# A fused two-block kernel: modulation work of the feed-forward stage regrouped between DVE and TensorE

## What is computed

```python
# first block (x: 256 x 2048, c: 2048)
mod = silu(c) @ w_ada + b_ada                      # 2048 x 12288
shift1, scale1, gate1, shift2, scale2, gate2 = split(mod, 6)
x = x + gate1 * (concat(s5(...), dilated_attention(...)) @ w_out)
h2 = rms(x, norm2_w) * (1 + scale2) + shift2
x = x + gate2 * ((silu(h2 @ w_ffn_gate) * (h2 @ w_ffn_up)) @ w_ffn_down)    # hidden width 5632
# second block, two layers: attention with a context, then a Fourier mixer
sh, sc, g = split(silu(c_2) @ ada_w_2[i] + ada_b_2[i], 3)                  # 2048 x 6144, i = 0, 1
sh_c, sc_c, g_c = split(silu(c_ctx_2) @ ada_w_2[0] + ada_b_2[0], 3)        # the context, i = 0 only
```

## Time and profile before

| | |
|---|---|
| median of 3 runs | 2595.99 us (2595.85 to 2597.74) |
| profiled execution | 2597.22 us |
| its span, first to last instruction | 2595.4 us |
| mean granted TensorE clock | 0.972 of 2.4 GHz |
| busy: PE / PEld / DVE / ACT / POOL | 2450.6 / 2078.1 / 1652.6 / 1031.9 / 216.2 us |
| moved by DMA | 589.46 MB, mean 227 GB/s |

### The profile page before, as it was taken

One profiled execution on the slowest core, in us unless ns is written; L12 is line 12 of the kernel. 1 busy time (PEld: TensorE's weight loads), 2 busy tenths in 40 slices (PEclk: granted clock), 3 DMA queues, 4 the chain that ended last, 5 costly groups with the idle time before them and its releaser, 6 DMA issues.

```text
span 2595.4 us, 38240 instructions
## 1 busy us (share of the span) xinstructions
PE 2450.6 (94%) x15542; PEld 2078.1 (80%) x15542; DVE 1652.6 (64%) x2005; ACT 1031.9 (40%) x1374; POOL 216.2 (8%) x193
## 2 busy tenths in 40 slices
PE   5899898989999999999999999999968999999995
PEld 1588675569888989888887888888758999999894
DVE  8654644457777788876677566455674484765547
ACT  2453663224333333333343454444423333334431
POOL 0136900011000000000010100000002000000000
PEclk8899899989999999999999999999989999999998
DMA  9853469977999999997553754334544685765551
GB/s 389 311 160 121 134 227 350 381 274 266 350 352 343 366 350 345 340 332 279 155 175 123 223 163 125 100 100 130 177 139 159 199 284 160 242 216 179 155 170 41
DMA packets 278063, 589.46 MB, mean 227 GB/s; under 512 B 20608, under 2 KB 29824, under 8 KB 276608
## 3 DMA queue, kind: packets, MB, share of 16 engines
q1 hardware_dynamic: 277888, 587.02, 65.8%
HBM read 584.85 MB, written 2.10 MB: 226 GB/s over the span
## 4 chain that ended last, share of the span: by engine, by line
PE 86%; DVE 5%; POOL 3%; DMA 3%; issue 2%; ACT 2%; SPq 0%; DVEq 0%; ACTq 0%; POOLq 0%
PE psum L218 12%; PE psum L206 12%; PE psum L219 12%; PE psum L220 12%; PE psum L208 12%; PE psum L207 12%; PE psum L278 4%; DMA start_slots<-in_w_ada 2%; POOL pool_scan_tmp L779 1%; PE psum L2406 1%; PE psum L1794 1%; DVE wlo L195 1%; POOL xacc L779 1%; PE psum L426 1%; PE psum L2382 1%
## 5 line engine op out<-in xcount | busy, mean ns | idle before, releaser
L195 DVE TENSOR_TENSOR wlo<-raw,whi 128x1024 fp32r<-128x1024 f32 (+2 forms) x728 | 881.9, 1228 | 628.6 <-ACT whi L189 626.8
L189 ACT CAST whi<-raw 128x1024 fp32r<-128x1024 f32 (+2 forms) x728 | 736.8, 1022 | 981.9 <-PE psum L220 458.4
L218 PE MATMUL psum<-hh,whi 128*128 128x256 f32 x2688 | 760.5, 283 | 4.9 <-DVE wlo L195 4.4
L220 PE MATMUL psum<-hl,whi 128*128 128x256 f32 x2688 | 750.9, 279 | 0.0
L219 PE MATMUL psum<-hh,wlo 128*128 128x256 f32 x2688 | 750.9, 279 | 0.0
L218 PEld LDWEIGHTS psum<-hh,whi 128*128 128x128 f32 x2688 | 507.7, 189 | 28.1 <-issue 25.9
L220 PEld LDWEIGHTS psum<-hl,whi 128*128 128x128 f32 x2688 | 510.8, 190 | 0.0
L219 PEld LDWEIGHTS psum<-hh,wlo 128*128 128x128 f32 x2688 | 506.7, 188 | 1.6 <-issue 1.0
L206 PE MATMUL psum<-whi,hh 128*128 128x512 f32 (+1 forms) x736 | 301.2, 409 | 17.2 <-DVE wlo L195 14.0
L208 PE MATMUL psum<-whi,hl 128*128 128x512 f32 (+1 forms) x736 | 290.3, 394 | 0.0
L207 PE MATMUL psum<-wlo,hh 128*128 128x512 f32 (+1 forms) x736 | 289.7, 394 | 0.0
(11 more groups left out here) (351 smaller groups left out, 2249.6 us busy)
## 6 DMA issues: line engine op xcount, KB each, us to landing
araw<-in_ada_w SPq DMA_DIRECT2D x128, 512.0 KB, 6.5
raw<-in_w_in_fourier SPq DMA_DIRECT2D x128, 512.0 KB, 3.9
raw<-in_w_ffn_gate SPq DMA_DIRECT2D x88, 512.0 KB, 10.9
raw<-in_w_ffn_up SPq DMA_DIRECT2D x88, 512.0 KB, 7.4
raw<-in_w_ffn_down SPq DMA_DIRECT2D x88, 512.0 KB, 10.6
raw<-in_w_in_attn SPq DMA_DIRECT2D x88, 512.0 KB, 4.4
araw<-in_w_ada SPq DMA_DIRECT2D x80, 512.0 KB, 6.7
start_slots<-in_w_ada SPq DMA_DIRECT2D x64, 512.0 KB, 8.2
```

The costliest lines, as they stand in the source:

```text
L189: nc.scalar.copy(whi[:, u % SPLITS, 0:kn, 0:w], raw[:, u % RING, 0:kn, 0:w]).then_inc(s_hi, 1)
L195: nc.vector.tensor_tensor(wlo[:, u % SPLITS, 0:kn, 0:w], raw[:, u % RING, 0:kn, 0:w], whi[:, u % SPLITS, 0:kn, 0:w].bitcast(F32), ALU.subt ...
L218: nc.tensor.matmul(o, h, hh[:, kt + k], start=(kt + k == 0 and f % 2 == 0), stop=False)
L220: ins = nc.tensor.matmul(o, h, hl[:, kt + k], start=False, stop=(kt + k == KT - 1 and f % 2 == 1))
```

## The change

1. A DVE pair is worked at its whole width: loads of one row block and 1024 columns (4 KB rows), and 16 operations of 128x1024 in place of 32 of 128x512. `ada_load` and `ada_sum` go by kt, two at each place of `ADA24`.
2. The last two-vector pair (pair 15: `ada_w_2[0]`, columns 3072 to 4095) moves from PE's rounds to DVE: two row blocks a step, after units 18 and 20 of steps 1 to 8, two operations each (one for each vector) into `acc2`, which lies in `lng`, free until the Fourier stage. Its loads are issued by SP at j = 20 and 23, into slots 2 and 3 of `ffn_slots`. PE keeps 3 rounds a step (j = 5, 11, 17), SP 6 slot loads (j = 2, 5, ..., 17).
3. The sums over partitions of the eight feed-forward pairs and of the two vectors become rows of bank 7, beside those of PE's rounds: `row_sum` issues four matmuls in the four column groups, stationary a 128x32 window of `onez` with a column of ones, moving 256 columns of the accumulator. `ada_reduce` for them has no bias step behind it (`ada_store` is left to the Fourier pairs); `dual_reduce` follows unit 23 of step 8.
4. One turn for all: set 3 has 18 rows in place of 8, the copy of ACT waits for the row sums too, and DVE stores the columns by six additions. In step 9 copy, turn and store move from j = 2, 4, 8 to j = 3, 5, 9.
5. Two Fourier pairs keep the old sum over partitions, but take the wide operations and loads. Three small memsets on POOL, a `sel` of 2 x 32, slot bookkeeping to fit.

In the diff the old bodies of the rewritten functions are left out; they stand above.

```diff
@@ -117,7 +117,8 @@
-    sel = sb(ctx, "select", [P, 2, 8])
+    sel = sb(ctx, "select", [P, 2, 32])
+    onez = sb(ctx, "ones_window", [P, 63])
@@ -226,33 +227,45 @@
-    PE_PAIRS = (0, 1, 2, 3, 4, 5, 6, 7, 8, 9, 12, 13, 14, 15)
-    PE_SETS = ((0, 4, 1), (4, 2, 1), (6, 4, 1), (10, 4, 2))
+    PE_PAIRS = (0, 1, 2, 3, 4, 5, 6, 7, 8, 9, 12, 13, 14)
+    PE_SETS = ((0, 4, 1), (4, 2, 1), (6, 4, 1), (10, 3, 2))
...
+    R_FFN = 80
+    SLOT_USES = (8, 20)
...
+    def ffn_slot(step, k):
+        s = 8 * step + k
+        return ffn_slots[:, s % 4], s_slot[4 + s % 4], 16 * (SLOT_USES[1] + s // 4 + 1)
...
+            t, landed, _ = slot(m)
+            if 8 <= m < 64 or 72 <= m < 160:
+                sp.wait_ge(s_aused, (m - 8) // 2 + 1)
+            elif m >= 160:
+                step, k = divmod(m - 160, 6)
+                if k < 2:
+                    if step:
+                        sp.wait_ge(s_aused, R_FFN + 3 * step)
+                elif k < 4:
+                    if step:
+                        sp.wait_ge(s_dual, 2 * step - 3 + k - 1)
+                else:
+                    sp.wait_ge(s_aused, R_FFN + 3 * step + 1)
...
@@ -278,7 +291,7 @@
-                                           stop=(pi == np_ - 1 and kt >= 14), tile_position=(0, 32 * g))
+                                           stop=(st < 3 and pi == np_ - 1 and kt >= 14), tile_position=(0, 32 * g))
@@ -286,6 +299,9 @@
+        if st == 3:
+            act.wait_ge(s_red, 8)
+            act.wait_ge(s_dred, 1)
@@ -295,8 +311,8 @@
-        np_, vectors = PE_SETS[st][1:]
-        n = 4 * (vectors - 1) + np_
+        np_ = PE_SETS[st][1]
+        n = 18 if st == 3 else np_
@@ -310,12 +326,16 @@
         if vectors == 2:
-            nc.vector.tensor_tensor(modx[:], psum[:, 7, n:2 * n], bias, ALU.add)
+            b0 = COLS["bada"].start
+            for o, row, k in ((modx[:, 0:n], 4, c0), (modx[:, 24:32], 17, 120), (modc[:, 80:96], 8, 80),
+                              (modc[:, 128:176], 10, 128), (modc[:, 120:128], 16, 120)):
+                w = o.shape[1]
+                nc.vector.tensor_tensor(o, psum[:, 7, 8 * row:8 * row + w], cols[:, b0 + k:b0 + k + w], ALU.add)
         nc.vector.tensor_tensor(modc[:, c0:c0 + n], psum[:, 7, 0:n], bias, ALU.add).then_inc(s_mcol, 1)
-    def dve_rank(q):
-        return q - 20 if q < 24 else q - 28
+    def pair_rank(q):
+        return (q - 20) // 2 if q < 24 else (q - 28) // 2
@@ -324,53 +344,89 @@
...
+        return w, c * CW
+    def ada_load(sp, q, kt):
+        w, c = ada_src(q)
+        n = 16 * pair_rank(q) + kt
+        if n < 4:
+            sp.wait_ge(s_aused, set_rounds(2))
+        else:
+            sp.wait_ge(s_acc, n - 3)
+        sp.dma_start(arawf[:, 1024 * (kt % 4):1024 * (kt % 4) + 1024],
+                     w[kt * P:(kt + 1) * P, c:c + 2 * CW]).then_inc(s_slot[kt % 4], 16)
+    acc = powers[:].rearrange("p a b -> p (a b)")
+    def ada_sum(dve, q, kt):
+        g = pair_rank(q)
+        if kt == 0 and g:
+            dve.wait_ge(s_red, g)
+        dve.wait_ge(s_slot[kt % 4], 16 * (SLOT_USES[1] + 4 * g + kt // 4 + 1))
+        c0 = 0 if q < 24 else 16
+        w, s = arawf[:, 1024 * (kt % 4):1024 * (kt % 4) + 1024], cond[:, c0 + kt:c0 + kt + 1]
+        if kt == 0:
+            ins = nc.vector.tensor_scalar(acc, w, s, None, ALU.mult)
+        else:
+            dve.wait_ge(s_acc, 16 * g + kt)
+            ins = nc.vector.scalar_tensor_tensor(out=acc, in0=w, scalar=s, in1=acc, op0=ALU.mult, op1=ALU.add)
+        ins.then_inc(s_acc, 1)
+    def row_sum(pe, a, row, stop=False):
+        for half in range(2):
+            for e in range(2):
+                g, cs = 2 * half + e, slice(2 * P * e, 2 * P * e + 2 * P)
+                ins = nc.tensor.matmul(psum[32 * g:32 * g + 32, 7, cs], onez[:, 31 - row:63 - row],
+                                       a[:, half * CW + 2 * P * e:half * CW + 2 * P * e + 2 * P], start=False, stop=stop,
+                                       tile_position=(0, 32 * g))
+        return ins
+    def ada_reduce(pe, q):
+        g = pair_rank(q)
+        pe.wait_ge(s_acc, 16 * (g + 1))
+        if g < 8:
+            row_sum(pe, acc, 8 + g).then_inc(s_red, 1)
+            return
+        if g > 8:
+            pe.wait_ge(s_mod, g - 8)
+        for j in range(8):
+            ins = nc.tensor.matmul(psum[:, 6, j:j + 1], acc[:, j * P:(j + 1) * P], ones[:, 0:1], start=True, stop=True)
+        ins.then_inc(s_red, 1)
+    def ada_store(dve, q):
+        dve.wait_ge(s_red, pair_rank(q) + 1)
+        bias = cols[:, COLS["bada"].start + 4 * q:COLS["bada"].start + 4 * q + 8]
+        nc.vector.tensor_tensor(modc[:, 4 * q:4 * q + 8], psum[:, 6, 0:8], bias, ALU.add).then_inc(s_mod, 1)
+    s_dual, s_dred = sem("two_vector_ops"), sem("two_vector_reduced")
+    def dual_load(sp, kt):
+        t, landed, _ = ffn_slot(kt // 2, 6 + kt % 2)
+        sp.wait_ge(s_aused, R_FFN + 3 * (kt // 2) + 2)
+        sp.dma_start(t, dram["ada_w_2"][0][kt * P:(kt + 1) * P, 3 * 1024:4 * 1024]).then_inc(landed, 16)
+    def dual_sum(dve, kt):
+        w, landed, count = ffn_slot(kt // 2, 6 + kt % 2)
+        dve.wait_ge(landed, count)
+        if kt:
+            dve.wait_ge(s_dual, kt)
+        for v in range(2):
+            s = cond[:, 16 + 16 * v + kt:17 + 16 * v + kt]
+            if kt == 0:
+                ins = nc.vector.tensor_scalar(acc2[:, v], w, s, None, ALU.mult)
...
+                ins = nc.vector.scalar_tensor_tensor(out=acc2[:, v], in0=w, scalar=s, in1=acc2[:, v],
+                                                     op0=ALU.mult, op1=ALU.add)
+        ins.then_inc(s_dual, 1)
+    def dual_reduce(pe):
+        pe.wait_ge(s_dual, 16)
+        row_sum(pe, acc2[:, 0], 16)
+        row_sum(pe, acc2[:, 1], 17, True).then_inc(s_dred, 1)
...
@@ -1533,14 +1587,16 @@
             if not H.fourier and c == 9 and j == 0:
-                sp.wait_ge(s_acc, 16 * 16)
+                sp.wait_ge(s_acc, 16 * 8)
                 sp.dma_start(actx, dram["ctx_2"][0].rearrange("(t p) n -> p t n", p=P)).then_inc(s_ctx, 16)
-            pos = ADA24 if n == 24 else ADA_AFTER
-            if q is not None and j in pos:
-                a = pos.index(j)
-                ada_load(sp, q + a // 4, a % 4)
-            if not H.fourier and 1 <= c <= 8 and j % 3 == 2:
-                slots_sp(sp, 160 + 8 * (c - 1) + j // 3, 160 + 8 * (c - 1) + j // 3 + 1)
+            if q is not None and j in ADA24:
+                for kt in range(2 * ADA24.index(j), 2 * ADA24.index(j) + 2):
+                    ada_load(sp, q, kt)
+            if not H.fourier and 1 <= c <= 8:
+                if j % 3 == 2 and j < 18:
+                    slots_sp(sp, 160 + 6 * (c - 1) + j // 3, 160 + 6 * (c - 1) + j // 3 + 1)
+                if j in (20, 23):
+                    dual_load(sp, 2 * (c - 1) + (j - 20) // 3)
@@ -1606,7 +1662,7 @@
             if not H.fourier and c == 9:
-                if j == 2:
+                if j == 3:
                     set_row_act(act, 3)
@@ -1701,9 +1757,10 @@
                 if not H.fourier and c == 9:
-                    if j == 8:
+                    if j == 9:
                         set_store_dve(dve, 3)
                     if j == 10:
+                        dve.wait_ge(s_mcol, 4)
                         gate_dve(dve, 1, 80, diag, 0, 2)
@@ -1725,13 +1782,14 @@
                 first_turn_dve(dve, H, j, j + 1)
-            pos = ADA24 if n == 24 else ADA_AFTER
-            if q is not None and j in pos:
-                a = pos.index(j)
-                ada_sum(dve, q + a // 4, a % 4)
+            if q is not None and j in ADA24:
+                for kt in range(2 * ADA24.index(j), 2 * ADA24.index(j) + 2):
+                    ada_sum(dve, q, kt)
+            if not H.fourier and not first and c <= 8 and j in (18, 20):
+                dual_sum(dve, 2 * (c - 1) + (j - 18) // 2)
         if H.fourier and first:
             hidden_up_dve(dve, H, 0)
-        if q is not None:
+        if q is not None and H.fourier:
             ada_store(dve, q)
@@ -1854,11 +1912,11 @@
                     hidden_dft1_pe(pe, H, c)
-            if not H.fourier and 1 <= c <= 8 and j % 6 == 5:
-                r = 80 + 4 * (c - 1) + j // 6
+            if not H.fourier and 1 <= c <= 8 and j in (5, 11, 17):
+                r = R_FFN + 3 * (c - 1) + j // 6
                 rounds_pe(pe, r, r + 1)
             if not H.fourier and c == 9:
-                if j == 4:
+                if j == 5:
                     set_turn_pe(pe, 3)
@@ -1868,8 +1926,10 @@
                 ctx_turn_pe(pe, j // 2 - 1)
-            if q is not None and j == (13 if first else 19):
+            if q is not None and j == 19:
                 ada_reduce(pe, q)
+            if not H.fourier and c == 8 and j == 23:
+                dual_reduce(pe)
         if H.fourier and first:
@@ -1894,6 +1954,7 @@
+    acc2 = lng[:].rearrange("p (v n) -> p v n", v=2)
@@ -2790,6 +2851,9 @@
+        nc.gpsimd.memset(onez[:, 0:31], 0.0)
```

(2 more changed lines are left out.)

## The result

| | before | after |
|---|---|---|
| median of 6 runs each, us | 2598.39 | 2611.63 |
| lowest to highest, us | 2595.85 to 2602.36 | 2607.69 to 2613.66 |
| profiled execution, us | 2597.2 | 2612.13 |
| PE busy, us | 2450.6 | 2463.0 |
| DVE instructions | 2005 | 1873 |

What follows compares the result with a forecast made beforehand. PE, busy 94% of the span, was taken to bound the kernel. Removing 23.7 us and adding 7.5 took 16.2 off the profiled 2597.2, giving 2581.0 us, or 2579.8 for the median; range 2571 to 2592.

Steps and rivals of the forecast that it cites:

- what leaves PE: Feed-forward steps: eight rounds at 1.19 us and eight pair reductions at 1.78 leave PE's queue, 23.7 us removed.
- what comes to PE: Ten row sums at 0.75 us each join PE's queue: 7.5 us, between 5.5 and 11.9; the turn about 0.
- DVE's part: DVE's feed-forward step goes from 57.9 to 59.3 us, within PE's 70.4, so it adds nothing.
- walk to unit 20: DVE's queue after unit 18: hidden_add ends at 753.4, PE starts unit 20 at 756.6, 3.2 us of cover.
- the landings: Dual loads in ffn_slots: median 9.3 us, longest 13.7; they cost nothing if under 13.9.
- the rest: Step 9's later copy and extra stores, start memsets and Fourier wide sums: 0 on the end, at most 0.7 us.
- The first rival: Cover at unit 20 partly fails as dual loads land later than 13.9 us; 1 us a step gives 2588; chance 0.08.
- the second rival: Dual loads land after 18 us, each feed-forward step loses 4.1 us, 33 in all: 2613 us; chance 0.04.
- The third: Row sum's column groups run one after the other, 2.1 us each, 13.5 more in ten: 2593 us; chance 0.04.
- the 357 of the forecast: DMA engines in a feed-forward step: the same bytes in 70.4 us make 357 GB/s, for 349 before.
- the fourth rival: Unexplained gate and up pace, 2.0 us a step: up to 8 steps gain (2564) or lose (2596); chance 0.10, half each way.
- warning that steps 7 and 8 could change length: Sign of being wrong: feed-forward steps 7 and 8, or the Fourier stage's steps, change length; no size given.

Runs made afterwards that it cites:

- b_shift448: The kernel before with 448 unused bytes a partition behind select, no instruction changed: 2627.54 us, ratio 1.0115 to before.
- a_pad64: The changed kernel with 64 unused bytes behind the ones window: 2583.29 us, ratio 0.9943 to before.
- a_both: The changed kernel with 64 unused bytes behind the ones window and 96 behind skip_columns: 2562.65 us, ratio 0.9864 to before.
- b_again: The kernel before, unchanged, executed again: 2598.0 us, ratio 0.9998 to before.
- b_w64: The kernel before with 64 unused bytes between raw and whi: 2598.29 us, ratio 0.9991 to before.
- b_shift64: The kernel before with 64 unused bytes behind select: 2627.48 us, ratio 1.0109 to before.
- a_pad384: The changed kernel with 384 unused bytes behind the ones window: 2612.77 us, ratio 1.0056 to before.
- a_home: The changed kernel with select and the ones window behind skip_columns, so hh and hl keep their old addresses: 2585.69 us, ratio 0.9947 to before.
- b_stage96: The kernel before with 96 unused bytes behind skip_columns, ahead of the stage's tensors alone: 2579.62 us, ratio 0.9933 to before.

## Why the prediction was wrong, by its own steps

Stages of the span in us, from one hidden product to another (step 1 begins at the second of eleven; the ninth ends step 8):

| stage | before | b_shift448 | after | a_pad64 | a_both |
|---|---|---|---|---|---|
| to the first | 627.8 | 633.2 | 634.2 | 628.0 | 630.6 |
| to the second | 43.3 | 45.4 | 46.7 | 44.6 | 44.7 |
| seven steps | 511.6 | 521.5 | 507.2 | 499.2 | 493.5 |
| two steps | 153.7 | 157.5 | 154.6 | 150.5 | 149.2 |
| to Fourier | 689.9 | 696.8 | 696.3 | 690.4 | 687.8 |
| Fourier | 518.4 | 520.5 | 520.5 | 518.4 | 504.1 |
| rest | 50.7 | 50.9 | 50.8 | 51.0 | 51.1 |

The first line also varies by itself: it is 630.0 in b_again, and 633.7 in b_w64, whose paces are those of before. The first of the seven steps of after is 73.36 us long and the other six 72.30: ahead of the hidden product on DVE stand two first products of 0.74 us in step 1, and two sums of 1.28 in each later step.

**The forecast of -16.2 us held, at equal pace.** b_shift448 and after both run at 118.65 ns: 2627.54 - 2610.94 = 16.6 us. A step goes from 74.50 to 72.30, 2.20 us, where 1.19 + 1.78 - 0.75 = 2.22 was written. At remainder 0 a step goes from 74.99 (b_shift64) to 72.79 (a_pad384), 2.20 again, and the time by 2627.48 - 2612.77 = 14.7 (on two chips). At 192 it is 12.3 to 14.7 (a_home and a_pad64 against 2598.0): there the two paces divide anew, with a mean over the feed-forward stage of 115.2 and 115.0 ns for 114.6, which takes back (115.2 - 114.6) x 4224 = 2.5 us and 1.7 us. So "what leaves PE", "what comes to PE", DVE's part with its walk to unit 20, the landings and "the rest" stand. The first rival (a cover that fails) and the second (landings of 18 us) didn't come: 4.0 us of cover, 12.4 us at most. That the second rival's 2613 us lies next to the measured 2611.6 is luck; nothing of its mechanism is in the trace. The third, column groups one after the other, would be 2.1 us for a row sum; it is 0.76. The rule of the Trainium skill (TensorE: Matmul & The Clock Gate, Part 3, The mechanism) that a weight load overlaps running matmuls only when the row group differs is not what this trace shows: behind the row sum, the weight load that starts at 765.43 us and takes 0.19 lies inside the matmul of 765.32 to 765.82, on the same rows. And the rule is one of weight loads; that it would put the four column groups one after the other was the prediction's own step. The DMA engines carried 348 to 353 GB/s, less than the 357 of the forecast, since the step was longer; a_both has 362.

**The step that failed is the pace of the matmuls that the edit doesn't touch.** The sum has no term for it, so it was put at nothing, and the fourth rival, "a pace that I can't explain", gave it 16 us at most. It came to some 29 us. The rival's rows were the right ones and so was its warning that steps 7 and 8 could change length, but it was sized and given its chance wrongly, in three ways.

- Its bound was 2.0 us a step for 8 steps, 16 us either way, worked out from the two paces that the trace of before happened to show. After has a third, 118.65 ns, slower than both. With the mean over each whole stage, the feed-forward stage's 4224 matmuls of this kind lose (118.64 - 114.59) x 4224 = 17.1 us. The Fourier stage's 3072, called the slower ones already, lose (118.67 - 117.02) x 3072 = 5.1 us more, since its first 50 us had run at the quick pace before. The second block's attention has another 768, which lose (118.63 - 115.87) x 768 = 2.1 us.
- It took only the gate and up matmuls. The 2208 that have hh or hl stationary, 2112 of them with 512 columns, outside the feed-forward and Fourier stages, went from 229.5 to 232.4 ns where they lie before 600 us, and from 229.0 to 232.5 from 1750 to 2000 us; taken as 3 ns for all it is 6.6 us. The down matmuls gave back (234.1 - 233.2) x 1824 = 1.6 us.
- It was given 0.10, half each way, as if chance redrew it. It could have been asked what fixes it: the diff has two lines that move hh, and b_again shows that one program has the same paces again.

17.1 + 5.1 + 2.1 + 6.6 - 1.6 = 29.3 us, of the 29.4 between 2598.4 - 16.2 = 2582.2 and 2611.6. That it fits so closely is in part luck, as the first stage varies by some us between executions. The test without counting is b_shift448: 29.5 us from bytes that nothing reads.

**What stays open.** Why the remainder counts, which part of the memory or of PE it meets, isn't shown; only that it does, and that the paces by remainder are not a smooth curve. Nor is it settled why at 192 two paces follow each other in one execution, though b_stage96 and a_both show that the place of what lies above `skip_columns` has a part in it.

## What to carry to other kernels

When an edit resizes or adds a tensor, list which tensors it moves and what PE reads against them, and compare the starts of untouched matmuls in both traces before judging the edit: a pace that moved everywhere is the layout, not the work. Where PE bounds a kernel, try a few unused 32-byte to 256-byte blocks ahead of one activation tensor and, on their own, ahead of each further one that PE reads. Here two of them with the edit made 1.4% against the kernel before, 1.9% against the edit as it was written, and one of them 0.7% without the edit. Which remainder is best differs between matmuls of 256 and of 512 columns, so count both. An edit that is to be measured for itself needs the tensors that stay to keep their places, as in a_home.

## What the hardware did that was not expected

- In these layouts the 256-column matmuls started 113.3 to 120.0 ns apart and the 512-column ones 227 to 234 ns, by the distance of activation and weight modulo 256 bytes of a partition. The granted clock was 1.00 from 640 to 1180 us in every one of the runs.
- 64 unused bytes made a kernel of 2598 us slower by 1.1% (b_shift64) or one of 2611 us quicker by 1.1% (a_pad64, 2583.29 / 2610.94).
- The duration of a 256-column matmul in the timeline is 0.28 us at each pace, and PE is busy without a gap at full clock at each; what tells is the distance of starts, or the count in a window.
- Rows of 4 KB in place of 2 KB lowered the packets from 278063 to 257581. The median landing in ffn_slots was 8.6 us after and 9.3 before, though its own rows had 4 KB in both; what shortened it, and whether it moved the time, no run separates.
